# Neighbourhood attention with its dense products put between the units of one stream

## The reference

```python
def na_mixer(h, hc, w_qkv, rpb, w_o, need_ctx):     # H = 16 heads of d = 64
    q = project_q(h)                                 # 512 tokens x 1024
    k, v = project_kv(h)
    kc, vc = project_kv(hc)                          # 256 context tokens
    y = neighbourhood_attention(q, k, v, kc, vc, rpb).reshape(B, S, H * d) @ w_o
```

```python
s = jnp.einsum('bjqhd,bmjnhd->bhjqmn', qr, kb) * scale          # 8 rows x 32 columns
s = jnp.where(col_valid, s + bias, NEG_INF_2)
s_ctx = jnp.einsum('bjqhd,bkhd->bhjqk', qr, kc) * scale         # 256 context keys
p = softmax_f32(jnp.concatenate([s_ctx, s], -1))
o = einsum(p[..., :n_ctx], vc) + einsum(p[..., n_ctx:], vb)
```

## Time and profile before

| | us |
|---|---|
| median of 3 runs (lowest, highest) | 4209.67 (4203.41, 4211.05) |
| the profiled execution | 4208.18 |
| its span | 4206.4 |
| busy PE / PE weight load | 3836.2 / 3169.8 |
| busy DVE / ACT / POOL | 2145.8 / 1390.8 / 1501.5 |

### The profile page before, as it was taken

One profiled execution on the slowest core, in us unless ns is written; L12 is line 12 of the kernel. 1 busy time (PEld: TensorE's weight loads), 2 busy tenths in 40 slices (PEclk: granted clock), 3 DMA queues, 4 the chain that ended last, 5 costly groups with the idle time before them and its releaser, 6 DMA issues.

```text
span 4206.4 us, 64441 instructions
## 1 busy us (share of the span) xinstructions
PE 3836.2 (91%) x25149; PEld 3169.8 (75%) x25149; DVE 2145.8 (51%) x3464; ACT 1390.8 (33%) x1880; POOL 1501.5 (36%) x494
## 2 busy tenths in 40 slices
PE   6999979999999987999999987899968888879997
PEld 5888868888888866888776666778758877657885
DVE  6344856444544576665454545876652322334232
ACT  3322343322422332322234441422244433324232
POOL 1344323443344331334420021444446533334441
PEclk9999989999999998999999998999989999999998
DMA  5454415444444332344211003244414422212321
GB/s 178 149 157 141 138 41 160 137 152 145 143 142 139 117 97 79 125 137 150 85 33 24 22 2 120 90 130 150 130 57 143 130 67 60 78 41 74 95 90 51
DMA packets 551814, 441.52 MB, mean 105 GB/s; under 512 B 60332, under 2 KB 549821, under 8 KB 551357
## 3 DMA queue, kind: packets, MB, share of 16 engines
q1 hardware_dynamic: 551613, 438.67, 33.7%
HBM read 431.58 MB, written 2.83 MB: 103 GB/s over the span
## 4 chain that ended last, share of the span: by engine, by line
PE 65%; DVE 14%; issue 13%; ACT 4%; POOL 2%; DMA 1%; SPq 1%; DVEq 0%; ACTq 0%; POOLq 0%
PE ps_all L1872 19%; PE ps_all L1874 19%; PE ps_all L1873 19%; DVE acc L2444 3%; POOL w_lo L791 2%; PE ps_all L1937 1%; DMA g_raw<-in_w_mod_dram 1%; DVE full_t L2501 1%; DVE stat L2397 1%; ACT w_hi L1208 1%; PE ps_all L1781 1%; ACT prob_n L1168 1%; PE ps_all L1863 1%; DVE unit_t L2488 1%; DVE prod_t L2519 1%
## 5 line engine op out<-in xcount | busy, mean ns | idle before, releaser
L791 POOL TENSOR_TENSOR w_lo<-raw,w_hi 128x2048 fp32r<-128x2048 f32 (+4 forms) x326 | 1339.6, 4110 | 2298.4 <-ACT w_hi L1208 2198.4
L1872 PE MATMUL ps_all<-h_hi,w_hi 128*128 128x512 f32 (+1 forms) x2704 | 1071.9, 396 | 45.2 <-POOL h_lo L797 34.7
L1208 ACT ACTIVATE w_hi<-raw 128x2048 fp32r<-128x2048 f32 (+4 forms) x320 | 537.7, 1681 | 1595.0 <-PE ps_all L1874 1422.8
L1873 PE MATMUL ps_all<-h_lo,w_hi 128*128 128x512 f32 (+1 forms) x2704 | 1057.6, 391 | 0.0
L1874 PE MATMUL ps_all<-h_hi,w_lo 128*128 128x512 f32 (+1 forms) x2704 | 1057.1, 391 | 0.0
L1872 PEld LDWEIGHTS ps_all<-h_hi,w_hi 128*128 128x128 f32 x2704 | 517.2, 191 | 158.0 <-issue 28.4
L2444 DVE SCALAR_TENSOR_TENSOR acc<-g_raw,c_col,acc 128x256 f32<-128x256 f32 x1104 | 618.5, 629 | 1.7
L1874 PEld LDWEIGHTS ps_all<-h_hi,w_lo 128*128 128x128 f32 x2704 | 516.5, 191 | 107.4
L1873 PEld LDWEIGHTS ps_all<-h_lo,w_hi 128*128 128x128 f32 x2704 | 517.9, 192 | 102.4 <-issue 1.0
L1872 PE MATMUL ps_all<-hid_hi,w_hi 128*128 128x512 f32 (+1 forms) x1272 | 481.3, 378 | 27.6 <-DVE hid_lo L2522 18.9
L1874 PE MATMUL ps_all<-hid_hi,w_lo 128*128 128x512 f32 (+1 forms) x1272 | 473.2, 372 | 0.0
(11 more groups left out here) (359 smaller groups left out, 5008.3 us busy)
## 6 DMA issues: line engine op xcount, KB each, us to landing
raw<-in_w_ffn_gu_dram SPq DMA_DIRECT2D x88, 1024.0 KB, 5.0
g_raw<-in_w_mod_dram SPq DMA_DIRECT2D x72, 1024.0 KB, 5.0
raw<-in_ffn_w_in_dram SPq DMA_DIRECT2D x66, 1024.0 KB, 5.0
g_raw<-in_ada_w_dram SPq DMA_DIRECT2D x48, 1024.0 KB, 5.3
raw<-in_w_ffn_down_dram SPq DMA_DIRECT2D x32, 768.0 KB, 4.7
raw<-in_w_ffn_down_dram SPq DMA_DIRECT2D x32, 640.0 KB, 4.3
raw<-in_ffn_w_out_dram SPq DMA_DIRECT2D x24, 768.0 KB, 4.7
raw<-in_ffn_w_out_dram SPq DMA_DIRECT2D x24, 640.0 KB, 4.2
```

What stands on the lines that cost most here:

```text
L791: nc.gpsimd.tensor_tensor(v(w_lo), v(raw), v(w_hi).bitcast(F32), ALU.subtract).then_inc(sem["w_split_lo"], 1)
L1208: nc.scalar.activation(w_view(w_hi, j % 2, st["shapes"][j]), w_view(raw, j % 2, st["shapes"][j]), ACT.Copy).then_inc(sem["w_split_hi"], 1)
L1872: nc.tensor.matmul(o, whi, mhi, start=first, stop=False)
L1873: nc.tensor.matmul(o, whi, mlo, start=False, stop=False)
```

## The change

The step `na` becomes one stream of 32 units, as the MLA step is.

- Weights are regrouped: 12 panels of 1024 KB. A panel `qk` holds 128 columns of Q and the 128 of K for one pair of heads, loaded by two DMAs; a panel `v` holds 256 columns of V, for four heads.
- The dense products are cut in 33 fills of one PSUM bank (`NA_PROLOGUE` and `na_fill`): Q of a pair (`q`), its K (`k`), its context K in half a bank (`kc`), or V of one token tile in half a bank (`v`). Six fills into six banks come first, one more behind the first scores. From then on the tensor engine's order in a round `u` is `scores(u+1)`, a fill into bank 7, `turn(u)`, `weigh(u-1)`; the last fill is in round 25. A fill waits until ScalarE has evacuated the one before.
- `nv` and `nvb` get second buffers; one lies in `hc`, which nobody needs any more.
- ScalarE's order in a round is `exps(u+1)`, the evacuation of the fill, `copy(u)`, `keep`, and `split_hi` of the panel two later when the round's fill was a panel's last. VectorE's is `most(u+1)`, `shares(u+1)`, `copy(u)`. GpSimd's is the biases of unit `u+2`, then a `split_lo`.
- The scaling by 1/8 goes into the evacuation of Q, so that the small multiply after the maximum goes (the maximum is negated in the same instruction), and the early scaling of the bias table goes too.
- The splits of `on_lat` move from `gather` into rounds 25 to 31, and the scaling of `x` to round 2 on VectorE.
- SP's order: the panels, biases and bands of a pass are issued in turn, and the projection's first two panels after the last biases.

```diff
+NA_PANELS = [("qk", 0), ("v", 0)] + [p for i in range(3) for p in (("qk", 2 * i + 1), ("v", i + 1), ("qk", 2 * i + 2))] + [("qk", 7)]
+def na_fill(u):
+    i, n = (u + 1) // 8, (u + 1) % 8
+    if i > 3 or i == 3 and n > 2:
+        return None
+    if i == 3 and n == 2:
+        return [("kc", 7)]
+    return [[("q", 2 * i + 1)], [("k", 2 * i + 1)], [("kc", 2 * i + 1), ("v", i + 1, 0)], [("v", i + 1, 1), ("v", i + 1, 2)],
+            [("v", i + 1, 3), ("v", i + 1, 4)], [("v", i + 1, 5), ("kc", 2 * i + 2)], [("q", 2 * i + 2)], [("k", 2 * i + 2)]][n]
+NA_PROLOGUE = [[("q", 0)], [("v", 0, 2), ("v", 0, 3)], [("v", 0, 4), ("v", 0, 5)], [("k", 0)], [("kc", 0), ("v", 0, 0)], [("v", 0, 1)]]
+NA_BANKS = [0, 2, 3, 1, 4, 5]
...
-    nv = sb("nv", [P, 6, PER * HD], at=spare)
-    nvb = sb("nvb", [P, 4, 2, PER * HD], at=tmp + 4096)
+    nv = (sb("nv_even", [P, 6, PER * HD], at=spare), sb("nv_odd", [P, 6, PER * HD], at=spare + 6144))
+    nvb = (sb("nvb_even", [P, 4, 2, PER * HD], at=tmp + 4096), sb("nvb_odd", [P, 4, 2, PER * HD], at=hc_at))
...
+                def biases(i, pair):
+                    if i:
+                        sp.wait_ge(sem["bias_made"], b["bias_made"] + i * 16 - 8 * (1 - pair))
...
+                def bands(i):
+                    sp.wait_ge(sem["fill_out"], b["fill_out"] + (8 * i + 4 if i else 3))
...
+                biases(0, 0)
+                biases(0, 1)
+                bands(0)
+                for i in range(3):
+                    load_panel(st, 0, 3 * i + 4)
+                    load_panel(st, 0, 3 * i + 5)
+                    biases(i + 1, 0)
+                    if i < 2:
+                        load_panel(st, 0, 3 * i + 6)
+                    bands(i + 1)
+                    biases(i + 1, 1)
                 early = st["following"]
+                load_panel(early, 0, 0)
+                load_panel(early, 0, 1)
...
+                made(0)
+                made(1)
+                for j in range(2):
+                    split_lo(ahead(st, 0, j, True))
+                for u in range(NA_ALL):
+                    if u + 2 < NA_ALL:
+                        made(u + 2)
+                    for part in na_fill(u) or ():
+                        if na_ends(part):
+                            split_lo(ahead(st, 0, na_panel(part), True))
+                    if u >= 25:
+                        h_low(b, u - 25, u - 25, S, on_lat[:, u - 25, :], (h_hi, h_lo))
+                h_low(b, KD - 1, KD - 1, S, on_lat[:, KD - 1, :], (h_hi, h_lo))
...
-                    nc.gpsimd.tensor_scalar(table[:, :, :], table[:, :, :], HD ** 0.5, None, ALU.mult).then_inc(sem["table_scaled"], 1)
...
+        for f, bank in enumerate(NA_BANKS):
+            fill_out(f, bank)
+            if f >= 4:
+                split_hi(ahead(st, 0, f - 4, True))
         exps(0)
+        fill_out(NA_FIRST, 7)
+        for u in range(NA_ALL):
+            if u + 1 < NA_ALL:
+                exps(u + 1)
+            fill_out(u + NA_FIRST + 1, 7)
+            copy(u)
+            if u % 4 == 0 and u:
+                keep(u - 1)
+            for part in na_fill(u) or ():
+                if na_ends(part):
+                    split_hi(ahead(st, 0, na_panel(part), True))
+            if u >= 25:
+                high(u - 25)
+        keep(NA_ALL - 1)
+        high(KD - 1)
...
+        for f, bank in enumerate(NA_BANKS):
+            if f in (0, 4):
+                pe.wait_ge(sem["h_ready"], b["h_ready"] - (0 if f else KD))
+            fill(f, bank)
         scores(0)
+        fill(NA_FIRST, 7)
+        for u in range(NA_ALL):
+            if u + 1 < NA_ALL:
+                scores(u + 1)
+            if na_fill(u) is not None:
+                pe.wait_ge(sem["fill_out"], b["fill_out"] + u + NA_FIRST + 1)
+                fill(u + NA_FIRST + 1, 7)
+            turn(u)
+            if u:
+                weigh(u - 1)
+        weigh(NA_ALL - 1)
...
-            ch.link(V.tensor_reduce(s_(n, 0), pair, AX_X, ALU.max))
-            V.tensor_scalar(s_(n, 1), s_(n, 0), -(HD ** -0.5), None, ALU.mult).then_inc(sem["s_max"], 1)
+            V.tensor_reduce(s_(n, 1), pair, AX_X, ALU.max, negate=True).then_inc(sem["s_max"], 1)
...
         most(0)
+        shares(0)
+        for u in range(NA_ALL):
+            if u + 1 < NA_ALL:
+                most(u + 1)
+                shares(u + 1)
+            copy(u)
+            if u == 2:
+                ch.link(V.tensor_scalar(x[:, :], x[:, :], ALPHA, None, ALU.mult))
```

More of the change, by code:

```diff
@@ L275, in norm_step, with na_parts, na_panel, na_ends @@
+NA_BANKS = [0, 2, 3, 1, 4, 5]
+def na_parts(f):
+    return NA_PROLOGUE[f] if f < NA_FIRST else na_fill(f - NA_FIRST - 1)
+def na_panel(part):
+    return NA_PANELS.index(("v" if part[0] == "v" else "qk", part[1]))
+def na_ends(part):
+    kind, n = part[0], part[1]
+    if kind == "v":
+        return part[2] == (5 if n else 1)
+    return kind == ("kc" if n % 2 or n == 0 else "k")
+def na_made(f):
+    return sum(1 for m in range(f + 1) if not na_ends(na_parts(m)[-1]))
 def norm_step(mode, A, B=None, N=S, ctx=False, dst="h", then=None, fused=False):
@@ L432, in build @@
     x = sb("x", [P, KD * S])
+    hc_at = place[0]
     hc = sb("hc", [P, KD * C])
@@ L845, in _, with made @@
-                one(0, False)
-                with pool.Fori(1, st["iters"] - 1) as i:
-                    one(i, False)
-                one(st["iters"] - 1, True)
+                def made(u):
+                    i, m = u // NA_N, u % NA_N
+                    pair, j = m // 4, m % 4
+                    if j == 0:
+                        pool.wait_ge(sem[f"bias_in{pair}"], b[f"bias_in{pair}"] + (i + 1) * (2 * 16 * ROWS))
+                    x0 = BAND[j] - j * QC + QC
+                    if u >= 2:
+                        pool.wait_ge(sem["s_biased"], b["s_biased"] + u - 1)
+                    for g in range(2):
+                        nc.gpsimd.tensor_tensor(bias_m[:, u % 2, g, :].rearrange("p (r n) -> p r n", n=KC_), bias_w[pair][:, g, :, x0:x0 + KC_],
+                                                na_mask[:, (0, 1, 1, 2)[j], :].rearrange("p (o n) -> p o n", o=1).broadcast_to([P, ROWS, KC_]),
+                                                ALU.add).then_inc(sem["bias_made"], 1)
@@ L1186, in na_act, with copy @@
-        exps(0)
-        for n in range(U):
-            if n + 1 < U:
-                exps(n + 1)
-            copy(n)
-            if n >= 2 and NA_UNITS[n - 2] == (0, 3):
-                keep(n - 2)
-        keep(U - 1)
+        def copy(u):
+            act.wait_ge(sem["turned0"], b["turned0"] + u + 1)
+            if u >= 2:
+                act.wait_ge(sem["s_weighted"], b["s_weighted"] + u - 1)
+            nc.scalar.activation(half_nt(u, 0), ps_all[:, 4, :].rearrange("p (u q) -> p u q", q=HD), ACT.Copy).then_inc(sem["copied0"], 1)
@@ new lines, in fill @@
+        def fill(f, bank):
+            parts = na_parts(f)
+            if parts is None:
+                return
+            for m, part in enumerate(parts):
+                panel = na_panel(part)
+                pe.wait_ge(sem["w_split_lo"], p0 + panel + 1)
+                whi, wlo = (w_view(t, panel % 2, st["shapes"][panel]) for t in (w_hi, w_lo))
+                ps, half_ps = ps_all[:, bank, :], ps_all[:, bank, m * C:(m + 1) * C]
+                for k in range(KD):
+                    x_in = [t[:, k * S:(k + 1) * S] for t in (h_hi, h_lo)]
+                    c_in = [t[:, k * C:(k + 1) * C] for t in (ch_hi, ch_lo)]
+                    first, last = k == 0, k == KD - 1
+                    if part[0] == "q":
+                        ins = triple(ps, whi[:, k, 0:P], wlo[:, k, 0:P], *x_in, first, last)
+                    elif part[0] == "k":
+                        ins = triple(ps, whi[:, k, P:2 * P], wlo[:, k, P:2 * P], *x_in, first, last)
+                    elif part[0] == "kc":
+                        ins = triple(half_ps, whi[:, k, P:2 * P], wlo[:, k, P:2 * P], *c_in, first, last)
+                    else:
+                        t = part[2]
+                        tok = [u[:, t * P:(t + 1) * P] for u in c_in] if t < 2 else [u[:, (t - 2) * P:(t - 1) * P] for u in x_in]
+                        ins = triple(half_ps, *tok, whi[:, k, :], wlo[:, k, :], first, last)
+                if na_ends(part):
+                    ins.then_inc(sem["panel_used"], 1)
+                elif m == len(parts) - 1:
+                    ins.then_inc(sem["fill_made"], 1)
@@ L1707, in scores, with turn @@
             ins.then_inc(sem["s_made"], 1)
[L1709 to L1714 removed]
+        def turn(u):
+            pe.wait_ge(sem["s_shared"], b["s_shared"] + u + 1)
+            for h in range(2):
+                pe.wait_ge(sem[f"copied{h}"], b[f"copied{h}"] + u)
             for g in range(2):
@@ L2048, in _ @@
             elif kind == "na":
-                for i in range(st["iters"]):
-                    na_pe(st, b, pe, triple, i)
+                na_pe(st, b, pe, triple)
             elif kind == "store":
```

275 lines of the change are left out of this document (99 added, 176 removed).

## The result

The changed kernel takes 4166.75 us (median of 4 runs, 4161.9 to 4170.58), the kernel before 4206.54 on the same chip (4 runs, 4203.32 to 4211.05): a ratio of 0.9904, 95% interval 0.9887 to 0.9921. The prediction was 4167 with a gain of 41 us; measured are 39.8.

The account below looks back on a forecast made before the run. Units were taken as bound by a chain that leaves the tensor engine idle. Terms 1.0 + 179.4 + 107.2 + 5.0 + 8.9 + 11.8 + 12.4 = 325.7 us against 366.9; 4209.67 - 41 = 4168, written as 4167, range 4151 to 4184.

Parts of the forecast that it names:

- What bounds: Neighbourhood step: a chain through several engines bounds the units, leaving the tensor engine idle; units take 4.27 us for 3.2 of work.
- Rounds: Units under fills: tensor engine is the bound, a round 8.97 us; fills 179.4 us and 32 units 107.2 in all.
- Start: Before the first fill: V's larger first panel and its high half on ScalarE cost 1 us (0 to 2).
- Third panel: Second pair's Q and K, split after fill 4: idle 3.5 us plus 1.5 at half clock, 5.0 (0 to 8).
- Stall in round 24: Projection panel issued late behind SP's band copies and biases holds ScalarE, then the tensor engine: 8.9 us.
- The end: Units 26 to 31 run at VectorE's 4.8 us, 8.8 idle, plus GpSimd 3 us late: 11.8 (8 to 18).
- The small multiply: Multiply after the maximum in each unit: dropping it saves nothing in the wait for the exponentials.
- Projection: After the last weighing: gather's 2.75 us go, and the first panel takes 12.4 us, 1.5 of it for half clock.
- The sum: First fill's start to the projection's first result: 325.7 us against 366.9 before, 41 us less.
- Rival 2: Fills wait for their one bank, bank 7, costing 27 to 54 us: middle 4200, cheap half 4190; chance 0.09.
- Rival 1: The late projection panel doesn't stall, so the 8.9 us stay won: 4158; chance 0.16.
- rivals 3 and 4: 3: clock falls in the stream, up to 4410, chance 0.03. 4: fills don't overlap units, 4202, 0.06 with other small outcomes.

Follow-up runs that it names:

- kernel without overlap: Changed kernel plus one wait: each fill in the stream starts only after VectorE has made the shares of the unit it could cover; 4340.87 us, ratio 1.0319.
- The opening: First six fills reordered and third panel split a fill sooner, against the changed kernel with SP issuing the projection's panels earlier; 4153.52 us, ratio 0.9866.
- maximum in two steps: Small multiply after the maximum put back, against the changed kernel with SP issuing the projection's panels earlier; 4158.84 us (one run).
- the kernel with the order of the last units changed: From unit 26 VectorE copies before shares, GpSimd's last large split one unit later, against the changed kernel with projection panels issued earlier; 4157.39 us, ratio 0.988.
- late split: Against the kernel with the order of the last units changed: GpSimd splits the projection's second panel's low part only behind the last output rows; 4148.85 us, ratio 0.9839.
- all edits: Changed kernel with the late split, SP's earlier issue of the projection's panels and the opening together; 4147.82 us, ratio 0.9841 to the kernel before.

## Why the prediction was right, by its own steps

- **What bounds.** Right. The tensor engine's idle time was what could be won: its waits fell by 36.0 us (58.3 to 22.3) in a stage that is 38.8 shorter, while its busy time stayed (3836.2 and 3836.5). The kernel without overlap shows that the gain hangs on the overlap.
- **Rounds.** 8.97 us predicted as the mean; 9.12 with two 256-column halves and 8.87 with 512 columns. The switch of 0.1 us from the MLA rows holds. Fills and units together come out 1.2 us above 286.6 (179.4 + 107.2), by what the other terms leave of 328.1.
- **Start.** +1.0 for the larger V panel: it didn't show. From VectorE's subtraction of the mean to the first fill it is 7.85 us before, 6.16 in the first execution after, 7.85 in the second.
- **Third panel.** 3.5 idle and 1.5 half clock predicted; 3.2 and 1.6. The opening removed both. The 1.6 can also be absent: one kernel had none behind the same pause (last part).
- **Stall in round 24.** This was the riskiest step, and right in place, cause and most of its size: 8.9 predicted, 10.1 idle (11.2 in the second execution). SP's copies took 21.9 us for 20.7, the bias rows 8.2 for 7.7. What I left out is the half clock behind it, 2.6 us: the term is 12.7, the largest miss of the sum (+3.8). I had charged half clock after the idle near the third panel and forgot it after a longer one.
- **The end.** Period 4.8 predicted, 4.68 measured; GpSimd's split 3 us late, 2.0 measured. Idle is 9.0 for 11.8, but one unit behind the longest wait ran at half clock (5.8 us for 3.2): 11.6 in all. That the total comes out is luck: the idle was taken 2.8 us too long, and the half clock, 2.6, was left out again. The prediction also took the diagonal at its usual length, and beside that split it took 1.0 us more. VectorE (columns as above; the last two adds 4.68 apart, answering):

```profile
3645.80 1.45 DVE L2467 TENSOR_TENSOR diag_n<-ident,stat 128x256 f32<-128x256 f32 x1
...
3649.85 0.70 DVE L2456 TENSOR_TENSOR ps_all<-ps_all,bias_m 128x512 f32<-128x512 f32 x1 [2.00 <-POOL bias_m L883]
...
3654.53 0.69 DVE L2456 TENSOR_TENSOR ps_all<-ps_all,bias_m 128x512 f32<-128x512 f32 x1
```

- **Projection.** It follows the last weighing straight, as predicted; its first panel took 11.2 us for 12.4, since no clock was lost there.
- **The small multiply.** "Saves nothing": right under fills, and 0.36 us a unit behind them, which costs next to nothing in the sum.
- **The sum.** From the first fill 328.1 against 324.7 (325.7 less the start's 1.0): units +1.2, third panel -0.2, stall +3.8, end -0.2, projection -1.2. So misses of +5.0 and, with the start, -2.6 cancel in part, and the closeness of the whole is partly luck. The gain of the whole, 37.6 us by the spans, is this 38.8 with 1.7 from the faster norm and less 2.8 that the norm starts late by (3351.68 against 3348.90). Neither is the change's doing: in the second execution of the same kernel the norm took 5.41 us as before and started at 3348.57. For the same reason no gain can be seen from the dropped scaling of the bias table, which the prediction had at nothing.
- **Sums in it that don't follow.** Added up, its bounds for the start, the third panel, the stall and the end give 4153 to 4181, where it says 4158 to 4178. Rival 2's 4200 and 4190 come out only if the stall's 8.9 us go at the same time (4158 with 27 to 54 more), which it doesn't say. The forecast rests on neither.

Rival 1 is refuted by the stall, rival 2 by the round of 9.1 us with no wait for the bank, rivals 3 and 4 by the full stretches at clock 1.00; the kernel without overlap shows what the last two would have looked like.

## What to carry to other kernels

When dense work is put into the gaps of a chain, read the queues that feed it next: here one DMA queue's order was worth 12 us, a second buffer 66 us, both found by adding up issue times per copy. Where the tensor engine pauses as it did here (3.2 us, 10.1 us), put the slower matmuls behind the pause into the sum too, as a range (0 to 2.6 us here). And when one engine's order is improved, look at what the other engines do beside it: from unit 26 on the same edit gave 1.4 us with a GpSimd split at its side and 7.5 without.

## What the runs showed of the hardware

**VectorE's diagonal is held by GpSimd's split.** The diagonal multiply reads two operands from SBUF. Alone it takes 0.42 us. Beside a split it took 1.45 in the last units of the change and 4.54 in the kernel with their order changed, and both times it ended 0.28 us after the split (3647.25 for 3646.97, 3631.43 for 3631.15). The instructions that read PSUM are not held: the 32 copies, maxima and adds of the stage keep their 0.69, 1.23 and 0.70 us, though more than ten such splits run in it. It is the change that brought this about. In the kernel before, where no split ran beside the diagonals, none of them was longer than 426 ns; in the stage of the change the 32 diagonals are busy 32.9 us, a mean of 1.03 each. Before, then after:

```profile
L2404 DVE TENSOR_TENSOR diag_n<-ident,stat x32: 424/424/426, 3411.6 to 3700.9; 128x256 f32<-128x256 f32 x32
...
L2467 DVE TENSOR_TENSOR diag_n<-ident,stat 128x256 f32<-128x256 f32 x32 | 32.9, 1028 | 1.1
```

(The first line gives the shortest, median and longest in ns, then the first and last start.) Two SBUF operands aren't needed. The small multiply of the maximum in two steps reads one tensor from SBUF; it took 0.33 us alone, and 2.87 beside the split, ending 0.03 us after it:

```profile
3628.04 4.51 POOL L836 TENSOR_TENSOR w_lo<-raw,w_hi 128x2048 fp32r<-128x2048 f32 x1 [13.27 <-ACT w_hi L1272]
...
3629.71 2.87 DVE L2464 TENSOR_SCALAR stat<-stat 128x2 f32<-128x2 f32 x1
```

Under the fills VectorE has room, so this is seen only where its chain sets the pace. The Trainium skill (SBUF — State Buffer, SBUF: two separate sides) says that VectorE and GpSimd take turns on a shared pair of ports, held for a whole instruction. On VectorE's side it names instructions in a two-port mode, and those with two SBUF inputs against a GpSimd instruction that reads SBUF. The trace agrees for the second kind: 0.42 became 4.54 beside GpSimd's 4.50, and moving the split away gave 0.42 again. The small multiply has one input; whether it ran in a two-port mode no run here shows.

**The clock after a pause.** Eight profiled executions have the pause of 3.20 or 3.21 us for the third panel, with the same fill behind it. In seven of them some 8 matmuls of this fill run at the lower level; in the kernel with the order of the last units changed none does. First the change, then that kernel:

```profile
3390.76 0.53 PE L1941 MATMUL ps_all<-h_hi,w_hi 128*128 128x512 f32 x1 [3.20 <-POOL w_lo L834]
...
3391.51 0.63 PE L1943 MATMUL ps_all<-h_hi,w_lo 128*128 128x512 f32 x1
```

```profile
3386.47 0.50 PE L1943 MATMUL ps_all<-h_hi,w_hi 128*128 128x512 f32 x1 [3.21 <-POOL w_lo L836]
3386.81 0.40 PE L1944 MATMUL ps_all<-h_lo,w_hi 128*128 128x512 f32 x1
```

That is the 1.6 us by which this kernel's first turn is early (48.10 us after the first fill for 49.70), in code that its edit doesn't touch.

**The norm's clock.** The same 16 matmuls ahead of the first fill took 3.72 and 5.41 us in the two executions of the changed kernel, 3.72 in that of the late split, and 6.70 in that of all edits:

```profile
3351.13 6.70 PE L2009 MATMUL ps_all<-squares,mean_m 128*128 128x256 f32 x16 [2.93 <-DVE hc L2549]
```

The idle ahead of them is 2.93 us in all four. What decides at which level they run stays open; it is 3 us that no edit made, and the reason why the stage is counted from the first fill.
